# RWKV chunks: every other pair of chunks crosses to the opposite array quarters

## What is computed

```python
def wkv7_scan(r, w, k, v, a_vec, b_vec):
    ...
    def step(state, inp):
        r_t, w_t, k_t, v_t, a_t, b_t = inp
        sa = jnp.einsum('bhvk,bhk->bhv', state, a_t)
        state = (state * w_t[:, :, None, :] + sa[..., None] * b_t[:, :, None, :]
                 + v_t[..., None] * k_t[:, :, None, :])
        return state, jnp.einsum('bhvk,bhk->bhv', state, r_t)
    ...

def rwkv_branch(z, mu_prev, mu_next, w0, w_up, a0, a_up, g_up, k_k, k_a, r_k, lnx_g, lnx_b):
    ...
    y_f = wkv7_scan(r_h, decay_h[:, :, 0], k_dir[:, :, 0], v_h, -kk, kk * a_h[:, :, 0])
    fl = lambda t: jnp.flip(t, axis=1)
    y_b = fl(wkv7_scan(fl(r_h), fl(decay_h[:, :, 1]), fl(k_dir[:, :, 1]), fl(v_h),
                       fl(-kk), fl(kk * a_h[:, :, 1])))
    y = y_f + y_b
    ...
    y = y * lnx_g.astype(f32) + lnx_b.astype(f32)
    ...
    return (y * g).astype(z.dtype)
```

## Time and profile before

| | us |
|---|---|
| three runs | 4396.34, 4391.77, 4390.82 |
| median | 4391.77 |
| span of the profiled execution | 4385.4 |
| its own time, with the 6.4 around the span | 4391.8 |
| TensorE busy in the span | 3981.4 (91%) |
| VectorE / ScalarE / GpSimd busy | 1484.2 / 1014.8 / 605.2 |

### The profile page before, as it was taken

One profiled execution on the slowest core, in us unless ns is written; L12 is line 12 of the kernel. 1 busy time (PEld: TensorE's weight loads), 2 busy tenths in 40 slices (PEclk: granted clock), 3 DMA queues, 4 the chain that ended last, 5 costly groups with the idle time before them and its releaser, 6 DMA issues. The chain is left out here.

```text
span 4385.4 us, 95413 instructions
## 1 busy us (share of the span) xinstructions
PE 3981.4 (91%) x41485; PEld 2616.4 (60%) x41485; DVE 1484.2 (34%) x2542; ACT 1014.8 (23%) x2416; POOL 605.2 (14%) x732
## 2 busy tenths in 40 slices
PE   8798999998999979999978999989999989997995
PEld 3343447884444468888854444469888934445774
DVE  2556321142212310000043666556566532212003
ACT  2200100031101212222242441034444311112333
POOL 1020000001010000000010002244444311000112
PEclk8899999999999989999989999989999999997997
DMA  6352311103112089999960001100000031125998
GB/s 239 125 189 72 117 58 39 38 1 70 34 50 85 34 333 389 397 396 393 396 216 20 9 2 53 34 2 4 3 3 4 4 106 44 61 71 189 388 390 315
DMA packets 233424, 588.67 MB, mean 134 GB/s; under 512 B 36456, under 2 KB 140807, under 8 KB 213224
## 3 DMA queue, kind: packets, MB, share of 16 engines
q1 hardware_dynamic: 192291, 462.88, 28.9%
q0 software_dynamic: 19120, 73.68, 4.8%
q10 hardware_dynamic: 21782, 48.74, 3.3%
HBM read 514.20 MB, written 71.05 MB: 133 GB/s over the span
## 5 line engine op out<-in xcount | busy, mean ns | idle before, releaser
L1663 PE MATMUL experts_bank<-experts_uT,ex_wu 128*64 128x96 f32 x9216 | 390.7, 247 | 26.0 <-PE experts_bank L1649 22.1
L1663 PEld LDWEIGHTS experts_bank<-experts_uT,ex_wu 128*64 128x64 f32 x9216 | 384.4, 138 | 42.7 <-issue 42.7
L1736 DVE TENSOR_TENSOR experts_hT<-experts_si,experts_bank 128x384 f32<-128x384 f32 (+1 forms) x68 | 31.3, 460 | 724.1 <-PE experts_bank L1663 724.1
L192 PE MATMUL vgproj_bank<-vg_w,mix_hT 128*128 128x256 f32 x1024 | 225.4, 382 | 11.1 <-DVEq L201 7.7
L192 PEld LDWEIGHTS vgproj_bank<-vg_w,mix_hT 128*128 128x128 f32 x1024 | 195.6, 192 | 41.4 <-DVEq L201 8.5
L1663 PE MATMUL experts_bank<-experts_uT,b2z_hT 128*64 128x96 f32 x4096 | 178.1, 248 | 25.8 <-DMA b2z_hT<-in_w 16.7
L1663 PEld LDWEIGHTS experts_bank<-experts_uT,b2z_hT 128*64 128x64 f32 x4096 | 172.7, 138 | 40.4 <-issue 40.4
L1649 PE MATMUL experts_bank<-mixed_T,experts_hT 128*32 128x256 f32 (+1 forms) x2592 | 193.9, 451 | 0.0
L2260 POOL TENSOR_TENSOR b2z_hT<-b2z_hT,rwkv_level 128x256 f32<-128x256 f32 x192 | 153.7, 832 | 163.0 <-DVE b2z_hT L2613 162.9
L2629 DVE TENSOR_TENSOR rc_xy<-rc_xy,rc_bank 128x256 f32<-128x256 f32 x288 | 120.7, 421 | 123.3 <-PE rc_bank L2274 117.6
L1649 PEld LDWEIGHTS experts_bank<-mixed_T,experts_hT 128*32 128x32 f32 x2592 | 110.4, 110 | 69.6
(11 more groups left out here) (576 smaller groups left out, 7200.8 us busy)
## 6 DMA issues: line engine op xcount, KB each, us to landing
ex_wu<-in_expert_w SPq DMA_DIRECT2D x72, 2048.0 KB, 17.1
mixed_T<-in_expert_w SPq DMA_DIRECT2D x36, 2048.0 KB, 18.8
b2z_hT<-in_w SPq DMA_DIRECT2D x64, 1024.0 KB
...
```

What stands on the lines that cost most here:

```text
L192: last = pe.matmul(bk[t][:, 0:width], xT[:, k, t * P:(t + 1) * P], wt[:, s, k, :], start=(k == 0), stop=(k == KT - 1))
L1663: last = pe.matmul(bk[2 + j][c:c + 64, h * BT:(h + 1) * BT], wu[:, s, j, k, h * P + c:h * P + c + 64], uT[:, s, k, :], start=(k == 0), sto ...
```

## The change

Chunks 2 and 3 of a step are now "crossed": their token rows lie in the opposite half of the partitions, so that in most products the two calls of `mm` go from rows 0 to 63 to partitions 64 to 127 and the reverse. The chunks are issued in the order SPREAD = (0, 2, 1, 3), and a direction's four banks are one PSUM tensor in which a crossed chunk goes to the next bank (`place`); copies take both banks at once (`both`). Crossed are `begin`, `turn_tokens`, `keyed`, `first_y`, p1, p2, w, qg, h0 and `intra`; straight remain `first_x`, p3, `turn_a` and the S chain.

With it come: the unit matrix of the first inverse accumulated in PSUM by products of `eye` (`one_x`, the end of `keyed`) instead of VectorE's add; the end decay as a diagonal `fall` that GpSimd makes (`fall_of`) and that the transposes of k and b and the addition to qg use, so that `hh` is one plain copy a direction and S's update a plain addition; `begin` of the next turn issued in steps 2 and 3 of the S chain; the part of Y within a chunk (`intra`) computed apart in steps 0 and 1, copied by ScalarE (`yi`), and added by VectorE at the next turn's start (`rows_out`). VectorE's scans move behind level 5, its row scaling into levels 1 to 4, ScalarE's gates to levels 2 to 5.

```diff
+SPREAD = (0, 2, 1, 3)
...
+        S = sb2("S", [2, CH])
...
+        bk = [m.stack.enter_context(nc.psum_tensor(f"rc_banks{d}", [P, 4, HALF], F32)) for d in range(2)]
...
+        crossed = lambda j: int(j >= J // 2)
...
+        def place(d, odd, j, lo, width=CH):
+
+            at = lo + j % 2 * width
+            return bk[d][:, 2 * odd + crossed(j), at:at + width]
...
+            def fall_of(g):
+
+                gp.wait_ge(decayed, 5 * g + 5)
+                gp.tensor_tensor(fall[:, g % 2, :, :], eyes(2 * J), elc[:, g % 2, :, :].to_broadcast([P, 2 * J, CH]), ALU.mult).then_inc(fallen, 1)
...
+                if s + 1 < TURNS:
+                    fall_of(s + 1)
...
-            def mm(out, lhsT, rhs, start=True, stop=True):
-
-                for hp in heads:
-                    last = pe.matmul(out[hp, :], lhsT[hp], rhs[hp], start=start, stop=stop)
+            def mm(out, lhsT, rhs, cross=0, start=True, stop=True):
+
+                for n, hp in enumerate(heads):
+                    last = pe.matmul(out[heads[n ^ cross]], lhsT[hp], rhs[hp], start=start, stop=stop)
...
+            def begin(g, d):
+
+                now = pr[:, g % 2, d, :, :]
+                pe.wait_ge(rowed, g + 1)
+                if g:
+                    pe.wait_ge(acs[d], count(ACT_O, g - 1, "yi"))
+                for x, lo in ((2, 0), (3, 256)):
+                    for j in SPREAD:
+                        last = mm(place(d, 0, j, lo, 2 * CH), at_j(now[:, x, :], j), at_j(now[:, 0:2, :], j), crossed(j))
+                last.then_inc(begun[d], 1)
...
+                def turn_tokens(d):
+
+                    at(dvs, DVE_O, d, "yp")
+                    pe.wait_ge(fallen, s + 1)
+                    for j in SPREAD:
+                        mm(place(d, 1, j, 0), at_j(now[:, d, 3, :], j), fall[:, s % 2, J * d + j, :], crossed(j))
+                    for j in SPREAD:
+                        mm(place(d, 1, j, 128), at_j(Z[:, 8 + p, toks(s, d)], j), eye, crossed(j))
+                    for j in SPREAD:
+                        last = mm(place(d, 1, j, 256), at_j(now[:, d, 2, :], j), fall[:, s % 2, J * d + j, :], crossed(j))
...
+                def one_x(d):
+
+                    at(dvs, DVE_O, d, "ATk")
+                    mm(bk[d][:, 0, 0:256], eye, eyes(J), stop=False)
...
+                def keyed(d):
+
+                    at(dvs, DVE_O, d, "ATk")
+                    at(acs, ACT_O, d, "bN")
+                    for j in SPREAD:
+                        mm(place(d, 1, j, 0), ark[d][:, j, 0, :], kv[d][:, 1, j, :], crossed(j))
+                    for c in range(2):
+                        mm(bk[d][:, 2 + c, 128:256], eye, eyes(2), c, stop=False)
...
+                def first_x(d):
+
+                    at(pos, POOL_O, d, "m0")
+                    for j in SPREAD:
+                        last = mm(bk[d][:, 0, j * CH:(j + 1) * CH], lev[d][:, 0, j, :], eye, start=False, stop=j == SPREAD[-1])
...
+                def first_y(d):
+
+                    at(pos, POOL_O, d, "m0")
+                    for j in SPREAD:
+                        last = mm(place(d, 1, j, 128), eye, lev[d][:, 0, j, :], crossed(j), start=False, stop=j in SPREAD[2:])
...
+                        at(*((acs, ACT_O, d, "x") if l == 1 else (dvs, DVE_O, d, f"x{l - 1}")))
+                        for j in SPREAD:
+                            last = mm(place(d, 0, j, 0), lev[d][:, l, j, :], xy[d][:, 0, j, :], crossed(j))
+                    elif part == 2:
+                        at(acs, ACT_O, d, "y" if l == 1 else f"p1_{l}")
                         if l > 1:
...
+                        for j in SPREAD:
+                            last = mm(place(d, 0, j, 0), xy[d][:, 1, j, :], p1[d][:, j, :], crossed(j))
+                    else:
+                        at(acs, ACT_O, d, "akv" if l == 1 else f"p1_{l}")
+                        if l > 1:
+                            at(dvs, DVE_O, d, f"xt{l - 1}")
+                        for j in SPREAD:
+                            last = mm(bk[d][:, 3, j * CH:(j + 1) * CH], p1[d][:, j, :], xy[d][:, 1, j, :])
...
+                def turn_a():
+
+                    pe.wait_ge(tanhed, 4 * min(s + 3, TURNS))
+                    for d in range(2):
+                        for j in SPREAD:
+                            last = mm(bk[d][:, 2, j * CH:(j + 1) * CH], at_j(now[:, d, 0, :], j), eye)
+                        last.then_inc(turned, 1)
...
+                def intra(d):
+
+                    at(acs, ACT_O, d, "h")
+                    for j in SPREAD:
+                        mm(place(d, 0, j, 0), arb[d][:, j, 1, :], w[d][:, j, 1, :], crossed(j), stop=False)
+                        last = mm(place(d, 0, j, 0), ark[d][:, j, 1, :], kv[d][:, 1, j, :], crossed(j), start=False)
+                    last.then_inc(within[d], 1)
...
+                turn_tokens(0)
+                one_x(0)
+                keyed(0)
+                turn_tokens(1)
+                first_x(0)
+                first_y(0)
                 level(0, 1, 1)
...
+                one_x(1)
+                first_x(1)
+                keyed(1)
+                first_y(1)
                 for l in range(1, 5):
                     level(0, l, 2)
+                    if l == 1:
+                        level(1, 1, 1)
...
+                    if l == 1 and s + 2 < TURNS:
+                        gate_logits(s + 2)
+                    if l == 3:
+                        turn_a()
...
+                    for j in SPREAD:
+                        last = mm(place(d, 0, j, 0, 2 * CH), xy[d][:, 1, j, :], xn(rw[d][:, j, :, :]), crossed(j))
...
+                        mm(bk[d][:, 3, j * CH:(j + 1) * CH], qg[d][:, j, 1, :], S[d][:, n % 2, :]).then_inc(pes[d], 1)
+                    for d in range(2):
+                        j = order(d)[n]
+                        last = mm(bk[d][:, 2, j * CH:(j + 1) * CH], qg[d][:, j, 0, :], S[d][:, n % 2, :])
                         if n == J - 1:
                             last.then_inc(pes[d], 1)
-                        mm(bj(bk[d][0], j), qg[d][:, j, 1, :], S[d][:, :]).then_inc(pes[d], 1)
+                    if n < 2:
+                        intra(n)
+                    elif s + 1 < TURNS:
+                        begin(s + 1, n - 2)
...
                 act.wait_ge(ready, g)
+                act.wait_ge(rowed, g)
...
+                if g >= 2:
+                    act.wait_ge(fallen, g - 1)
...
+                    if l in (2, 3) and s + 2 < TURNS:
+                        gate(s + 2, l - 2)
...
+                for d in range(2):
+                    at(pes, PE_O, d, "h0")
+                    act.activation(halves(hh[d][:, :, :]), both(d, 0, 0, 128), ACT.Copy).then_inc(acs[d], 1)
+                for d in range(2):
+                    act.wait_ge(within[d], s + 1)
+                    act.activation(halves(yi[d]), both(d, 0, 0, 128), ACT.Copy).then_inc(acs[d], 1)
...
+                    if s:
+                        rows_out(s - 1, d).then_inc(dvs[d], 1)
...
+                    dve.wait_ge(begun[d], s + 1)
+                    for to, lo in ((arb[d][:, :, 0:2, :], 0), (ark[d][:, :, :, :], 256)):
+                        dve.tensor_tensor(to.rearrange("p (h j) x n -> p h j (x n)", h=2), both(d, 0, lo, lo + 256).rearrange("p h (j n) -> p h j n", j=2), mask,
+                                          ALU.mult).then_inc(dvs[d], 1)
...
+                    if s + 1 < TURNS and l < 5:
+                        scale_row(s + 1, l - 1)
...
+                    if s + 2 < TURNS:
+                        scan(s + 2, x)
...
+                    dve.tensor_tensor(pairs4(qg[d][:, :, 1, :]), turned_in[:, :, :, 1, :], pairs4(fall[:, s % 2, J * d:J * d + J, :]), ALU.add).then_inc(dvs[d], 1)
...
-                        dve.scalar_tensor_tensor(S[d][:, :], bj(bk[d][0], j), elc[:, s % 4, d, j:j + 1], hh[d][:, j, :],
-                                                 ALU.mult, ALU.add).then_inc(dvs[d], 1)
...
+                        dve.tensor_tensor(S[d][:, (n + 1) % 2, :], bk[d][:, 3, j * CH:(j + 1) * CH], hh[d][:, j, :], ALU.add).then_inc(dvs[d], 1)
```

284 lines of the change are left out of this document (127 added, 157 removed).

## The result

The changed kernel takes **4350.75 us** (4340.1 to 4360.91, four runs) against 4391.77 before: a ratio of 0.9905, with a 95% interval of 0.9888 to 0.9921. It is faster by 41 us. The prediction was 4260, with 4350 as the upper end of its range, so the time lies just outside the range and the gain is a third of the forecast one.

The account below looks back on a forecast made before the run. TensorE's matmul pace was taken to bound the chunk phase's turns; plain turns falling from 35.0 to 26.2 us save 142 us in 16, less 7 for late masks and 4 at the start: -131, 4260 us, range 4210 to 4350.

Parts of the forecast that it names:

- Part 1, four abreast: Chunk phase, TensorE: crossed 64-column records start every 14.6 ns instead of 29.1, so 22.5 us a turn instead of 32.3.
- Part 2, the chain of 26.2 us: Chunk phase, plain turn: head, middle and tail of waits and copies through the engines take 26.2 us instead of 35.0.
- its terms of the tail: End of a plain turn: w, copy, qg and h0, VectorE adds, S steps and the wait for two begins, 7.7 us.
- the sum at the end of part 2: Plain turn: 25.5 us of chain, 0.4 for restarts, 0.25 for late masks: 26.2, saving 8.9 a turn, 142 in 16.
- Rival B: Chunk phase, TensorE: matmul starts have a floor of 29.1 ns, so only 19 us faster, 4373; chance 0.13.
- B's other estimate: The same rival with the Trainium skill's floor of about 25 ns a start: 28.5 us of TensorE, some 4336.
- the eight loads in 0.06 us: Evidence from L1649: 8 weight loads began within 0.06 us, so loads were taken not to queue behind each other.
- I charge no clock: Chunk phase: turns with pauses already show granted clock 1.00, so new pauses were priced at nothing.
- Rival D: Chunk phase: side engines become the bound, GpSimd's masks start late; a turn of some 29 us, -96, 4296; chance 0.17.
- the cover the prediction named: Chunk phase: GpSimd idles 12.9 us a turn before the level masks, so the new `fall_of` costs nothing.
- Rival C: Chunk phase, TensorE: crossed pairs wait for straight ones, 34.8 us a turn against 32.3, +40, 4432; chance 0.08.

Follow-up runs that it names:

- onehead: The changed kernel with only one head's share of most products issued from the second turn on, half of the instructions: 4372.96 us, ratio 0.9985.
- after_again: The changed kernel itself, unchanged, measured a second time: 4339.45 us, ratio 0.989.
- straight: The changed kernel with the crossing undone, every product from a half to the same half, all other edits kept: 4423.4 us, ratio 1.0089.

## Why the prediction was wrong

- **Part 1, four abreast: right.** Crossed groups of 16 start 0.23 us apart and straight ones (p3) still 0.45, and TensorE's busy time fell by 116 us. By the prediction's sum it would be 9.8 us in 16 turns, 157; a busy row counts more than starts, so the two compare only roughly.
- **The Trainium skill's rule against the change** (TensorE: Matmul & The Clock Gate, Part 3, "The mechanism": a load overlaps only another row group) doesn't hold here: crossed and straight calls share their row groups, and 16 records start in 0.23 us.
- **Part 2, the chain of 26.2 us: nearly right.** onehead's plain turns at full clock take 26.9 us. The 0.7 us are 11 us in 16 turns. It was sized as a chain of waits and copies, and for plain turns this part of the argument stands (its terms of the tail add up to 7.8, not 7.7, which changes nothing).
- **The step that failed** is the sum at the end of part 2. It says that with TensorE off the bound "the chain through the engines does" fill the turn, and that was taken as the only thing left. TensorE has a third limit beside its array and its waits: the rate at which instructions reach it. It was hidden as long as a record took 29.1 ns, and a pace of 14.6 uncovers it. The term was zero in the sum and measures 61 us of late starts in the phase.
- **Rival B was the right question with the wrong figure.** It noted that "no sustained stretch of small records beats 29 ns" and made a floor for every start of that, at 29.1. What is measured is a price for a block, 3.43 us or 26.8 ns a matmul in the mean, while starts inside a block follow each other at 14.6. Put into B's own sum: 1008 x 26.8 ns + 1.8 = 28.8 us of TensorE, 3.5 us less than before, 56 in 16 turns, 4336; the two measurements are 4339 and 4351. That it comes so near is in part luck, since this sum has neither the long multiplies nor the chain in it. (B's other estimate, 28.5 us of TensorE, gives 3.8 x 16 = 61 us and so 4331, not the 4336 that stands beside it.) B got 0.13 because the eight loads in 0.06 us were taken to speak against it. They speak only against a floor per start: L1649 is a loop, whose instructions hardly had to come in again (last section).
- **The clock and VectorE: priced at nothing, in four turns not nothing.** "I charge no clock" held in plain turns (1.00). By the trace's list of granted clocks the phase has 58.0 us at the 0.50 level in after, 44.4 in after_again and 41.0 in before, 27.3 of each at its start. Of after's other 30.7 us, 23.9 begin within 3.3 us of the end of one of the four long multiplies, behind which TensorE had waited; the rest is less than before had. So in after the clock fell where VectorE was held up, and the two are one loss: 13 us in three turns, 4.3 each, by which an estimate for all four is 17 us. Step 1 gained nothing for this reason (40.3 to 40.1 us); without such a multiply the same turn took 35.2 in after_again.
- **Rival D: not as the bound, but its mechanism came.** GpSimd's masks take 789 ns each and TensorE waits for them 5.3 us in the whole phase, so GpSimd isn't what turns wait for. But D also said that VectorE's pair scaling and GpSimd "then slow each other", and that is what the long multiplies show, in four turns of 16 and not in each. The idle time before the masks shrank from 163.0 to 22.8 us, so the cover the prediction named is nearly used up. The first two rows are after's masks and `fall_of`, priced at 0.8 to 1.28 us; the third is TensorE's wait for the masks:

```profile
L2279 POOL TENSOR_TENSOR b2z_hT<-b2z_hT,rwkv_level 128x256 f32<-128x256 f32 x192 | 144.9, 789 | 22.8 <-DVE b2z_hT L2738 22.1
...
L2231 POOL TENSOR_TENSOR rc_fall<-rwkv_eye,rc_elc 128x512 f32<-128x512 f32 x16 | 17.0, 1062 | 0.0
```

```profile
PE rc_banks L2295 <- POOL b2z_hT L2279: 5.3, 6, 1.7
```

- **Rival C: no**, but its price was near: with crossed records never abreast of straight ones it gave +40, and straight, which uses two quarters only, came out at +37 (4423.4 against 4386.7 there).

In sum, 94 us of phase are missing in after (131 forecast, 37 come): 61 are pauses of the supply, some 17 the long multiplies with the clock behind them (an estimate from three turns), 11 the chain. The three were measured apart, and no run shows that they simply add; some 5 us are left over. In after_again, with one long multiply, 81 are missing.
